# A one-core hybrid retention and latent-attention layer: the order of the first loads and of the first tile's products

## What is computed

```python
h = rmsnorm(x, mix_norm_g)
z = h @ w_in              # columns: 4 x 512 for retention, then 256 + 128 + 64 latent
ret = retention(rq, rk, rv, rg, positions)     # 4 heads, chunks of 64
att = mla(c_q, c_kv, k_pe, positions, ...)     # 4 heads, low-rank q and kv
x = x + concat(ret, att) @ w_o
h = rmsnorm(x, ffn_norm_g)
x = x + (silu(h @ w_ffn_gate) * (h @ w_ffn_up)) @ w_ffn_down
x = x + sigmoid(rmsnorm(x, ple_norm_g) @ w_ple_gate) * (p @ w_ple_proj)
return rmsnorm(x, final_norm_g)
```

## Time and profile before

| what | value |
|---|---|
| median of 3 runs | 1248.72 us (1248.57 to 1248.84) |
| the profiled execution's own time | 1248.54 us |
| its span, first to last instruction | 1246.7 us |
| PE busy | 1233.4 us (99%) |
| DVE, POOL, ACT busy | 719.9, 514.3, 483.8 us |
| mean granted clock of TensorE | 0.998 |
| moved by DMA | 115.09 MB, mean 92 GB/s |

### The profile page before, as it was taken

The page is one execution under the profiler, slowest core; times in us unless marked ns, Lnnn a source line. Parts: engine busy times, 40 slices in busy tenths (PEclk is TensorE's granted clock), DMA queues, the critical chain, the costliest instruction groups (busy, mean ns, idle before and its releaser), DMA issues.

```text
span 1246.7 us, 16762 instructions
## 1 busy us (share of the span) xinstructions
PE 1233.4 (99%) x6006; PEld 1040.8 (83%) x6006; DVE 719.9 (58%) x1172; ACT 483.8 (39%) x892; POOL 514.3 (41%) x515
## 2 busy tenths in 40 slices
PE   9999999999999999999999999999999999999997
PEld 8888888888898888888888888888888888888886
DVE  5544444466664437845444445444499999954433
ACT  7622222256664225533333333333354344424422
POOL 2533343351110003555533455433499889810011
PEclk9999999999999999999999999999999999999999
DMA  9511101000021500243332342422555545420002
GB/s 343 165 35 49 36 2 43 1 18 18 17 104 50 152 1 1 76 127 101 111 121 71 105 127 85 127 90 80 186 199 157 169 169 189 149 85 1 1 34 101
DMA packets 101931, 115.09 MB, mean 92 GB/s; under 512 B 4832, under 2 KB 67680, under 8 KB 101856
## 3 DMA queue, kind: packets, MB, share of 16 engines
q1 hardware_dynamic: 101424, 113.57, 28.0%
q10 hardware_dynamic: 432, 0.54, 0.1%
HBM read 90.49 MB, written 23.59 MB: 92 GB/s over the span
## 4 chain that ended last, share of the span: by engine, by line
PE 96%; DVE 2%; ACT 1%; issue 1%; DMA 0%; POOLq 0%; DVEq 0%; SPq 0%; POOL 0%; ACTq 0%
PE PS L1749 11%; PE PS L1750 11%; PE PS L1748 11%; PE PS L206 8%; PE PS L208 8%; PE PS L207 8%; PE PS L2082 5%; PE PS L2084 5%; PE PS L2083 5%; PE PS L1043 3%; PE PS L1059 3%; PE PS L2461 2%; PE PS L2460 2%; PE PS L2459 2%; PE PS L871 2%; PE PS L2474 2%
## 5 line engine op out<-in xcount | busy, mean ns | idle before, releaser
L206 PE MATMUL PS<-WF,HTH 128*128 128x512 f32 (+1 forms) x448 | 176.5, 394 | 0.2 <-DVE HTL L436 0.2
L208 PE MATMUL PS<-WF,HTL 128*128 128x512 f32 (+1 forms) x448 | 173.3, 387 | 0.0
L207 PE MATMUL PS<-WF,HTH 128*128 128x512 f32 (+1 forms) x448 | 172.9, 386 | 0.0
L1469 DVE TENSOR_TENSOR X<-X,PS 128x512 f32<-128x512 f32 x172 | 110.2, 678 | 54.4 <-PE PS L208 37.3
L1748 PE MATMUL PS<-HTH,WF 128*128 128x512 f32 x336 | 130.7, 389 | 0.0
L1749 PE MATMUL PS<-HTL,WF 128*128 128x512 f32 x336 | 130.7, 389 | 0.0
L1750 PE MATMUL PS<-HTH,WF 128*128 128x512 f32 x336 | 130.7, 389 | 0.0
L1681 DVE TENSOR_TENSOR WF<-RAW,WF 128x512 fp32r<-128x512 f32 x63 | 70.9, 1126 | 77.5 <-ACT WF L1671 77.5
L1748 PE MATMUL PS<-WF 128*128 128x512 f32 x252 | 98.0, 389 | 0.0
L1749 PE MATMUL PS<-WF 128*128 128x512 f32 x252 | 98.0, 389 | 0.0
L1750 PE MATMUL PS<-WF 128*128 128x512 f32 x252 | 98.0, 389 | 0.0
(11 more groups left out here) (266 smaller groups left out, 2808.0 us busy)
## 6 DMA issues: line engine op xcount, KB each, us to landing
hid<-TMP SPq DMA_DIRECT2D x74, 256.0 KB, 2.3
TMP<-hid SPq DMA_DIRECT2D x25, 512.0 KB, 4.4
RAW<-in_w_ffn_gate SPq DMA_DIRECT2D x22, 512.0 KB, 4.2
RAW<-in_w_ffn_up SPq DMA_DIRECT2D x22, 512.0 KB, 5.4
RAW<-in_w_ffn_down SPq DMA_DIRECT2D x22, 512.0 KB, 4.2
X<-in_x SPq DMA_DIRECT2D x16, 512.0 KB, 5.7
RAW<-in_w_in SPq DMA_DIRECT2D x32, 256.0 KB, 3.6
TAB<-hid SPq DMA_DIRECT2D x9, 512.0 KB, 4.6
```

Source lines behind the costliest of these rows:

```text
L206: nc.tensor.matmul(dst, HTH[:, k, tok], w_h, start=(k == 0), stop=False)
L207: nc.tensor.matmul(dst, HTH[:, k, tok], w_l, start=False, stop=False)
L208: last = nc.tensor.matmul(dst, HTL[:, k, tok], w_h, start=False, stop=(k == K - 1))
L1469: nc.vector.tensor_tensor(x, x, src, ALU.add).then_inc(done, 1)
```

## The change

The first tile's turned rows come in two loads of four slices each, and the first weights in eight loads of one slice each instead of four of two, with the second half of the rows between the fourth and the fifth. Each of the eight has a semaphore of its own: `s_raw` for even slices, `s_rawb` for odd ones (so later waits on `s_rawb` count 16 more), and `s_ident` counts the second half of the rows (so its later wait counts 16 more). ACT and DVE take weights slices 0 to 3 before the second half of the rows, and split the second tile in two halves. PE has a loop of its own for the first tile, in which high·low, which needs the low half of the weights, is third and not second, and each matmul waits for just what it reads. And SP waits, behind the load of the second tile's turned rows, until these have landed, before it issues anything else.

```diff
+            def weights(k):
+                a = k % 2 * MLA_IN
+                e.dma_start(raw(k // 2)[:, a:a + MLA_IN],
+                            w[:, k, 4 * HALF:4 * HALF + MLA_IN]).then_inc((s_rawb if k % 2 else s_raw)[k // 2], 16)
+
+            def turned_half(k, arrived_half):
+                e.dma_start(rows_turned(0)[:, k:k + 4], t_in["x_turned"][0][:, k:k + 4]).then_inc(arrived_half, 16)
+            turned_half(0, s_e[0])
+            for k in range(4):
+                weights(k)
+            turned_half(4, s_ident)
+            for k in range(4, K):
+                weights(k)
             turned(1)
+            e.wait_ge(s_e[1], 16)
             rows(0)
             turned(2)
...
             high(0, 0, 4)
             slices(0)
+            slices(1)
             high(0, 4, 4)
-            slices(1)
             slices(2)
             slices(3)
-            high(1)
+            high(1, 0, 4)
+            high(1, 4, 4)
...
+            def first_tile(dst):
+                for k in range(K):
+                    w_h, w_l = big(1, 0, k, MLA_IN), big(1, 1, k, MLA_IN)
+                    if k % 4 == 0:
+                        e.wait_ge(n_mix.hi, k // 4 + 1)
+                    e.wait_ge(w_hi if k % 2 else w_even_hi, k // 2 + 1)
+                    nc.tensor.matmul(dst, HTH[:, k, 0:P], w_h, start=(k == 0), stop=False)
+                    if k % 4 == 0:
+                        e.wait_ge(n_mix.lo, k // 4 + 1)
+                    nc.tensor.matmul(dst, HTL[:, k, 0:P], w_h, start=False, stop=False)
+                    e.wait_ge(w_lo if k % 2 else w_even_lo, k // 2 + 1)
+                    last = nc.tensor.matmul(dst, HTH[:, k, 0:P], w_l, start=False, stop=(k == K - 1))
+                return last
```

More of the change, by code:

```diff
@@ L197, in mixed_lo, with product @@
             last.then_inc(w_lo, 1)
-        def product(dst, tile, slot, n=HALF, before=None):
+        def product(dst, tile, slot, n=HALF):
             tok = slice(tile * P, tile * P + P)
             for k in range(K):
-                if before:
-                    before(k)
                 w_h, w_l = big(slot, 0, k, n), big(slot, 1, k, n)
@@ L342, in high @@
             def high(t, k=0, n=K):
-                e.wait_ge(s_e[t % 4], 16 * (t // 4 + 1))
+                if t == 0 and k:
+                    e.wait_ge(s_ident, 16)
+                else:
+                    e.wait_ge(s_e[t % 4], 16 * (t // 4 + 1))
                 d = slice(t * P, t * P + P)
@@ L347, in slices @@
             def slices(c):
-                arrived(e, c)
                 for i in range(2):
+                    e.wait_ge((s_rawb if i else s_raw)[c], 16)
                     a = 8192 + c * 1024 + i * HALF
@@ L372, in act_1 @@
                     arrived(e, M_RET + c)
-                    e.wait_ge(s_rawb[c], 16)
+                    e.wait_ge(s_rawb[c], 32)
                     mixed_hi(GK, 0, c, raw(c))
@@ L446, in dve_1 @@
             slices(0)
+            slices(1)
             low(0, 4, 4)
-            slices(1)
             slices(2)
             slices(3)
-            low(1)
+            low(1, 0, 4)
+            low(1, 4, 4)
             for t in range(T):
@@ L497, in pe_1 @@
             idle_products(18)
[L499 to L505, removed]
+            def first_tile(dst):
[11 more added lines that the diff above has]
+                return last
+            first_tile(bank(LAT_AT[0], MLA_IN)).then_inc(lat_done, 1)
+            for t in range(1, T):
+                e.wait_ge(n_mix.lo, 2 * t + 2)
+                product(bank(LAT_AT[t], MLA_IN), t, 1, MLA_IN).then_inc(lat_done, 1)
         z_proj, z_out = sem("z_proj"), sem("z_out")
@@ L653, in pe_2 @@
         def pe_2(e):
-            e.wait_ge(s_ident, 16)
+            e.wait_ge(s_ident, 32)
             for s in range(NR + 3):
@@ L731, in act_2 @@
                     arrived(e, M_RET + 4 + 4 * head + c)
-                    e.wait_ge(s_rawb[c], 16 * (head + 2))
+                    e.wait_ge(s_rawb[c], 16 * (head + 3))
                     mixed_hi(GK, (head + 1) % 2, c, raw(c))
@@ L1497, in act_4 @@
             for c in range(4):
-                e.wait_ge(s_rawb[c], 16 * (HEADS + 1))
+                e.wait_ge(s_rawb[c], 16 * (HEADS + 2))
                 granule_hi(e, 0, c, M_WO1 + c)
```

## The result

| | before | after |
|---|---|---|
| median (range), 8 runs each | 1248.82 us (1248.57 to 1249.36) | 1252.92 us (1251.80 to 1254.98) |
| the profiled execution's own time | 1248.54 us | 1253.69 us |
| its span | 1246.7 us | 1251.9 us |

The ratio is 1.0034, interval 1.0024 to 1.0043: the change costs 4.1 us. The forecast was 1250.4, with a range of 1248.8 to 1251.6, and the time lies above it. The eight times after fall in two groups, 1251.80 to 1252.30 (4 runs) and 1253.54 to 1254.98 (4 runs); the first have a mean granted clock of 0.999, the second 0.996 to 0.998. The profiled execution is of the second. Two single executions, at 1372.03 and 1546.64 us, both in kernels of the experiments with whole first rows, had a mean granted clock of 0.85 and 0.75 and are left out here.

What follows compares the result with a forecast made beforehand. PE was taken as the bound, with a DMA, ACT, DVE chain 0.44 us ahead of it at the first head; a 2.25 us stream lag moved the head from 47.34 to 49.2, so 1248.54 + 1.86 = 1250.4, range 1248.8 to 1251.6.

Steps and rivals of the forecast that it cites:

- So rows of tile 4 land 2.25 us later: DMA stream: tile 4's rows 2.25 us late, so the last low part at the first head comes at 49.15, not 46.90.
- Halved loads and new order at the start: Kernel start: ACT's 0.41 us hole for the first weights goes, so PE's second tile starts at 12.78, not 13.19.
- Five more issues ahead of the second tile's rows: SP's queue: that load is issued near 5.8, not 3.31, yet still lands at 10.6; costed at nothing.
- Low half third on PE: PE's first tile: 0.4 us of matmuls end earlier, ahead of a wait that ends later anyway; gain nothing.
- The new wait on SP: SP's later loads start at 10.6 on empty engines; stream 2.25 us late, not made good, PE stands about 2.1 us.
- The price of an empty queue: Landing of 512 KB on empty engines: 3.5 us by the trace's row; 3.2 by the skill's rule, giving 1250.1.
- Sum: PE's start of the first head moves from 47.34 to 49.2, +1.86 us, giving 1250.4; ends 1250.0 and 1250.8.
- Rival A: PE's stall at about 47 us lowers its clock, costing 2.4 us more: 1252.8; chance 0.12 with its milder form.
- Rival B: DMA lag at tile 4 stays under 0.4 us and is hidden, so PE's side decides: 1248.3; chance 0.08.
- C: Only half the 2.25 us DMA lag is left: +0.7 us, 1249.3; chance 0.12.

## Why the prediction was wrong

The mechanism was the one forecast: the wait drains the stream, the rows of tile 4 come late, ACT and DVE come late with them, and PE stands before the head. The size of the lag was off, in two terms of the sum: the landing of the second tile's rows, costed at nothing, was 1.15 us late, and "So rows of tile 4 land 2.25 us later" left out 0.2 us of drain and 0.8 us behind it. That PE's hole came out as forecast (2.1, measured 2.20) is luck: PE was to be ready at 47.1 and to start at 49.2, and both came some 2.1 us later, PE itself because its second tile and tile 2 started late and its matmuls ran at the slower cadence (last section). By its steps:

- **Halved loads and new order at the start.** ACT started earlier (3.56, where the step kept 4.72, as the gains landed earlier), but its hole for the weights did not go: it stood 1.27 and 0.31 us for them. And the second tile started at 13.80, not 12.78: it waited for its rows, which landed at 11.75. The engines' side of this step holds (12.70 and 12.77 with whole rows and no wait); the landing fails.
- **Five more issues ahead of the second tile's rows.** This was costed at nothing, and it is the first term that failed: +1.15 us. The issue itself was where I had it (5.44, against "near 5.8"); the sum assumed that bytes in front move at the same 386 GB/s, and they moved at 354. Over 7.2 us that is 0.23 MB, or 0.6 us; the rest fell between 10 and 12 us, where the engines' share was 0.13. Halving the first rows explains 0.6 to 0.9 of it without the wait (11.2 and 11.55, against 10.65 with whole rows). With eight weights loads the wait itself went with a later landing (11.75 against 11.2, 11.86 against 10.65), though that load is issued ahead of it; with four it did not (11.45 against 11.55, 10.5 against 10.6). Of these only 11.86 against 10.65 is beyond the spread of single traces. Why, stays open. My upper end for the landing, 10.9, was too near.
- **Low half third on PE.** Nothing, as forecast.
- **The new wait on SP.** The drain, taken by itself, was right: 2.25 us forecast, 2.25 measured where the second tile's rows landed at 10.5; 2.45 in the changed kernel. What the step left out is a further loss where the small loads pass, 0.8 us here and 1.05 in the kernel with the wait alone: they pass at 105 to 184 GB/s there and at 142 to 194 here, where it was 340 before. "There is no slack in it in which to catch up" held, but the stream did not stay full: the share fell to 0.61 here at 20 us, and where it was 0.93, with the wait alone, the engines moved 105 GB/s. That the short lead of these loads is the reason is argued, not shown. The step did see that later issues wait for `squares`; with the small loads moved away, the lag that is left seems to come through there.
- **The price of an empty queue.** The rule of the Trainium skill, page "DMA: Bandwidth & Descriptors" (a fixed part of about 2.0 us beside the bytes, section "Anatomy of one DMA", which overlaps other work if the load is issued early, section "Rules for kernel authors"), gives as an estimate 3.2 us for 512 KB. The trace doesn't bear the figure out, but is near: the measured landings on empty engines were 3.5 to 3.6 us, so the row was the better price.
- **Sum.** Forecast lag 2.25, measured 4.4; head +1.86 forecast, +4.07 measured. Head +4.07 less 0.7 at the end (last section) is +3.3 to +3.4, and the runs that kept their clock are at 1251.80 to 1252.30, 3.0 to 3.5 above before.
- **Rival A** got a chance of 0.12 for what then happened in half of the runs. Against it I had "2.1 us is short" and no row with a hole that long, which is no evidence. Its price was 1.6 us in the profiled execution, not 2.4, and 2.9 in that of the kernel with four loads; the changed kernel's slowest run, 1254.98, would fit the second. The median over both groups is the measured 4.1 above before.
- **Rival B and C** did not happen: no lag was hidden, and the gap was larger than forecast, not smaller.

What an account of the profiled execution gives, from the starts of PE's work: the head +4.07; the clock 1.6; the last matmul +5.89 (1238.12 before, 1244.01 after), the rest, 0.2, in between; and from the last matmul to the end of the span 8.6 us before, 7.9 after: +5.2.

## What to carry to other kernels

A wait put into a full DMA stream costs its drain (here 2.25 us), plus what is issued too late behind it, and any buffer that a late load frees late passes the drain on; if the wait has to stand there, small loads go in front of it, and here gave back 2 of 3 us. Price a stream's lag by bytes over the rate of the same transfers at the same lead, not by "the engines are full". And where a forecast makes a hole on PE longer than any the trace shows, the clock is a case with, here, an even chance, not an outsider.

## What the runs showed of the hardware

- **The clock.** Three traces show the granted clock at 0.50 (1.2 GHz) around a hole of PE, which was busy on both sides. After a hole of 2.20 us it fell 1.5 us behind the hole's end and stayed 3.4 us; after 2.43, 1.1 us behind it, for 3.4 us; with 2.60 it fell inside the hole, 1.9 us after PE had gone idle, and stayed 6.8 us. The traces with the wait alone (2.20) and with whole rows (2.69) keep 1.00, and so does the one with idle products in the hole. Told by their times, it fell in 4 of 8 runs of the changed kernel, 3 of 7 with the wait alone, 4 of 6 with four loads, perhaps 2 of 4 with whole rows and likely all 5 with the split first. After holes of 1.56 us and 1.16 us (11 runs each) no time points to it; the two high runs behind a hole of 0.78 us stay unexplained. The Trainium skill, page "TensorE: Matmul & The Clock Gate", Part 1, has the clock fall after idling; the trace agrees in kind.
- **Halved rows.** A first tile loaded in two halves of 256 KB went with 325 to 363 GB/s from 2.5 to 9.7 us, one of 512 KB with 372 to 391.
- **The end of the kernel.** The last store, 256 KB from ACT's queue, landed in 3.2 us before and in 2.5 after, and that takes 0.7 us off the end. Before, then after:

```profile
out_rows<-RAW ACTq DMA_DIRECT2D x1, 256.0 KB, 3.2
```

```profile
out_rows<-RAW ACTq DMA_DIRECT2D x1, 256.0 KB, 2.5
```

It is 2.4 or 2.5 us in all 11 kernels with the changed early loads and 3.2 in all 7 with those of before, the wait making no difference, nor the engines' code. In those seven one transfer of instructions stands in the last 9 us, but so it does in the two kernels with four weights loads, whose store took 2.4 and 2.5. The cause stays open. It is why the kernels without the wait are no slower than before though their head comes up to 0.5 us later.
- **Two cadences.** The 448-column matmuls start every 0.2026 us in some executions and every 0.2067 in others, all through the tiles of one execution. Four of the 18 profiles have the slow one, among them the changed kernel's; that of before has the fast one. Over the 168 matmuls of tiles 1 to 7 that is 0.7 us; that it is why the runs of the kernel before fall in two groups (up to 1248.9 and from 1249.2) is argued, not shown.
